# A gated decoder layer on one core: six seven-product places in each half of the down stage with activation sums kept for the second half, and two in each half of the output stage

## What is computed

```python
x = x + merged @ w_out[i]                      # 2048 x 2048
h2 = rms_norm(x, ln_ffn_w[i])
u = causal_depthwise_conv(h2 @ w_up[i], conv_w[i], conv_b[i])
u_gate, u_val = jnp.split(u, 2, axis=-1)
x = x + (jax.nn.silu(u_gate) * u_val) @ w_down[i]   # 5504 x 2048
h3 = rms_norm(x, ln_ple_w[i])
x = x + jax.nn.sigmoid(h3 @ w_ple_gate[i]) * (p[i] @ w_ple[i])
```

## Time and profile before

| | |
|---|---|
| median of 3 runs | 1422.91 us (1422.76 to 1422.95) |
| profiled execution | 1423.26 us, of it 1421.5 us from the first to the last instruction (its span) |
| TensorE matmuls busy | 1411.3 us, 99% of the span |
| VectorE busy | 1088.8 us, 77% |
| ScalarE busy | 793.7 us, 56% |
| mean granted TensorE clock | 0.999 |

### The profile page before, as it was taken

One profiled execution on the slowest core, in us unless ns is written; L12 is line 12 of the kernel. 1 busy time (PEld: TensorE's weight loads), 2 busy tenths in 40 slices (PEclk: granted clock), 3 DMA queues, 4 the chain that ended last, 5 costly groups with the idle time before them and its releaser, 6 DMA issues.

```text
span 1421.5 us, 19857 instructions
## 1 busy us (share of the span) xinstructions
PE 1411.3 (99%) x7054; PEld 1199.0 (84%) x7054; DVE 1088.8 (77%) x1386; ACT 793.7 (56%) x965; POOL 133.5 (9%) x87
## 2 busy tenths in 40 slices
PE   9999999999999999999999999999999999999997
PEld 7888888888888888888888888888888888888886
DVE  7676767878787888777777777777777888888887
ACT  7565665555455555465555555555555555554654
POOL 0024124100000000001110101101011000000000
PEclk9999999999999999999999999999999999999999
DMA  9655565565665665475656566566665565565663
GB/s 321 204 179 162 162 192 150 162 186 177 201 204 186 219 237 197 157 222 179 194 178 198 185 189 192 177 196 186 192 192 178 199 201 198 173 209 205 215 221 120
DMA packets 190733, 273.48 MB, mean 192 GB/s; under 512 B 11728, under 2 KB 103120, under 8 KB 190544
## 3 DMA queue, kind: packets, MB, share of 16 engines
q1 hardware_dynamic: 190096, 272.04, 59.8%
q10 hardware_dynamic: 576, 0.63, 0.1%
HBM read 270.53 MB, written 2.10 MB: 192 GB/s over the span
## 4 chain that ended last, share of the span: by engine, by line
PE 98%; DVE 1%; DMA 0%; ACT 0%; issue 0%; DVEq 0%; ACTq 0%
PE aux L996 11%; PE main L996 11%; PE main L744 9%; PE main L745 9%; PE main L746 9%; PE aux L1005 6%; PE main L802 6%; PE main L803 6%; PE main L804 6%; PE main L1005 6%; PE aux L802 4%; PE aux L804 4%; PE aux L803 4%; PE aux L745 2%; PE aux L744 2%; PE aux L746 2%
## 5 line engine op out<-in xcount | busy, mean ns | idle before, releaser
L1638 DVE TENSOR_TENSOR w_lo<-raw,w_hi 128x1024 fp32r<-128x1024 f32 (+1 forms) x476 | 581.1, 1235 | 272.4 <-ACT w_hi L1304 271.6
L1304 ACT ACTIVATE w_hi<-raw 128x1024 fp32r<-128x1024 f32 (+1 forms) x476 | 499.4, 1051 | 453.6 <-PE main L746 100.3
L744 PE MATMUL main<-w_hi,xT 128*128 128x512 f32 x446 | 175.8, 394 | 0.3 <-DVE w_lo L2215 0.3
L745 PE MATMUL main<-w_lo,xT 128*128 128x512 f32 x446 | 173.7, 389 | 0.0
L746 PE MATMUL main<-w_hi,xT 128*128 128x512 f32 x446 | 173.6, 389 | 0.0
L996 PE MATMUL aux<-xT,w_hi 128*128 128x512 f32 x704 | 169.7, 391 | 0.0
L996 PE MATMUL main<-xT,w_hi 128*128 128x512 f32 x672 | 162.8, 391 | 0.0
L996 PEld LDWEIGHTS aux<-xT,w_hi 128*128 128x128 f32 x704 | 129.4, 188 | 25.0
L996 PEld LDWEIGHTS main<-xT,w_hi 128*128 128x128 f32 x672 | 123.2, 188 | 23.6
L2340 POOL TENSOR_TENSOR act<-cv 128x512 f32<-128x512 f32 (+1 forms) x22 | 71.8, 3266 | 418.5 <-DVE cv L1880 418.5
L744 PEld LDWEIGHTS main<-w_hi,xT 128*128 128x128 f32 x446 | 83.8, 188 | 17.7 <-DVE xT L1665 1.2
(11 more groups left out here) (381 smaller groups left out, 2250.2 us busy)
## 6 DMA issues: line engine op xcount, KB each, us to landing
raw<-in_w_up SPq DMA_DIRECT2D x336, 256.0 KB
raw<-in_w_in SPq DMA_DIRECT2D x136, 512.0 KB
raw<-in_w_down SPq DMA_DIRECT2D x84, 512.0 KB
raw<-in_w_out SPq DMA_DIRECT2D x32, 512.0 KB
raw<-in_w_ple_gate SPq DMA_DIRECT2D x32, 512.0 KB
raw<-in_w_branch_a SPq DMA_DIRECT2D x16, 512.0 KB
raw<-in_w_branch_b SPq DMA_DIRECT2D x16, 512.0 KB
raw<-in_w_in SPq DMA_DIRECT2D x15, 256.0 KB, 5.8
```

The source lines that it names most:

```text
L744: pe.matmul(acc, th, wh, start=first, stop=False)
L745: pe.matmul(acc, th, wl, start=False, stop=False)
L1304: ac.activation(w_hi[:, u % RING, :, 0:w], raw[:, u % RING, :, 0:w], ACT.Copy).then_inc(hi_full, 1)
L1638: dve.tensor_tensor(w_lo[:, u % RING, :, 0:w], raw[:, u % RING, :, 0:w], w_hi[:, u % RING, :, 0:w].bitcast(F32), ALU.subtract).then_inc(lo ...
```

## The change

- The down stage has places at i = 6, 8, 11, 13, 15, 17 in either half: six where there were five.
- The six activation sums of the first half are kept in buffers of their own (`more_sums_hi`, `more_sums_lo`, 16 KB a partition) and used again in the second half, where none are made.
- The output stage has places at i = 2 and 4 in both halves, with the same two activation sums; before, the second half had i = 3 alone.
- In a VectorE slot the low parts of the weight sums come ahead of `act_sums`.
- In the first unit of an output place the product into `main` comes first, then the wait for the turned block and the product into `aux`. VectorE's low parts of the second turned block ("x1T1") move ahead of the `split_lo` of their slot.
- SBUF: the reserved descriptor scratch goes from its default to 1024 bytes a partition, the filler tile from 312 to 56 floats, to make room.

```diff
-SEVEN_AT = ((5, 8, 11, 14, 17), (5, 8, 11, 14, 17))
+SEVEN_AT = ((6, 8, 11, 13, 15, 17),) * 2
-OUT_AT = ((2, 4), (3,))
+OUT_AT = ((2, 4), (2, 4))
-OUT_FORMS = [2, 4, 3]
+OUT_FORMS = [2, 4]
-        + [DOWN_FORMS + q for q in range(len(SEVENS) - N_GATES - N_OUTS)])
+        + [DOWN_FORMS + SEVEN_AT[p].index(i) for p in range(2) for i in SEVEN_AT[p]]
+        + [DOWN_FORMS + len(SEVEN_AT[0]) + f for f in range(len(LAST_AT))])
-FILL = 312
+FILL = 56
+        more_sums_hi = sb("more_sums_hi", [P, 4, 4, P], F32R, ffn)
+        more_sums_lo = sb("more_sums_lo", [P, 4, 4, P], F32R, ffn)
...
                 if a == 0:
+                    triple(main[:, 0, 0, :], *m_block_t(2 * i + 1, 0), *ring_tile(u, 1), start=False, stop=False)
                     if first:
                         if p:
                             pe.wait_ge(xT_ready, 4 * (NQ + 2))
                         else:
                             pe.wait_ge(gated, 4 * NQ)
-                    triple(gate_product(0), *m_block_t(2 * i, 0), *ring_tile(u, 0), start=first, stop=end)
-                    mm = triple(main[:, 0, 0, :], *m_block_t(2 * i + 1, 0), *ring_tile(u, 1), start=False, stop=False)
+                    mm = triple(gate_product(0), *m_block_t(2 * i, 0), *ring_tile(u, 0), start=first, stop=end)
...
+                if s == out_slot(1) + 1 + X1_LAG[1]:
+                    lo_blocks("x1T1", xT_lo, xT_hi, 4, VCOL["ln_ffn"] + 4, xT_hi_ready, xT_ready, 4 * (NQ + 1))
...
+                for k in range(2):
+                    if s - k in SEVEN:
+                        sums_lo(SEVEN[s - k], k + 1)
                 if s in SUMS_AT:
                     act_sums(SUMS_AT[s])
                 if s + 2 in SEVEN:
                     weight_diffs(s + 2)
                 if s - 1 in SUMS_AT and s - 1 != FIRST_FORM_AT:
                     sums_lo(SUMS_AT[s - 1], 0)
-                for k in range(2):
-                    if s - k in SEVEN:
-                        sums_lo(SEVEN[s - k], k + 1)
...
-    nc = bacc.Bacc("TRN2", target_bir_lowering=False, num_devices=1)
+    nc = bacc.Bacc("TRN2", target_bir_lowering=False, num_devices=1, dynamic_dma_scratch_size=1024)
```

More of the change, by code:

```diff
@@ L158 @@
 SEVEN = {u: q for q, u in enumerate(SEVENS)}
-OUT_FORMS = [2, 4, 3]
+OUT_FORMS = [2, 4]
 DOWN_FORMS = len(GATES_AT) + len(OUT_FORMS)
 FORM = ([f for n in range(1, NQ) for f in range(len(GATES_AT))] + [len(GATES_AT) + OUT_FORMS.index(i) for p in range(2) for i in OUT_AT[p]]
-        + [DOWN_FORMS + q for q in range(len(SEVENS) - N_GATES - N_OUTS)])
+        + [DOWN_FORMS + SEVEN_AT[p].index(i) for p in range(2) for i in SEVEN_AT[p]]
+        + [DOWN_FORMS + len(SEVEN_AT[0]) + f for f in range(len(LAST_AT))])
 N_FORMS = FORM[-1] + 1
 SUMS_AT = {MIX + 2 * UK - 5 + 3 * f: f for f in range(len(GATES_AT))}
-SUMS_AT.update((WOUT + at, len(GATES_AT) + f) for f, at in enumerate([-12, -9, 12]))
-SUMS_AT.update((max(u - 4, DOWN + UK), FORM[q]) for u, q in SEVEN.items() if DOWN <= u < GATE)
+SUMS_AT.update((WOUT + at, len(GATES_AT) + f) for f, at in enumerate([-12, -9]))
+SUMS_AT.update((max(u - 4, DOWN + UK), FORM[q]) for u, q in SEVEN.items() if DOWN <= u < DOWN + 2 * UD)
 SUMS_AT.update((GATE + at, N_FORMS - len(LAST_AT) + f) for f, at in enumerate([6, 10]))
@@ L480, in form_place @@
         def form_place(f):
+            if DOWN_FORMS + 2 <= f < N_FORMS - len(LAST_AT):
+                return f - DOWN_FORMS + 1
             return 2 if f == 2 else f % 2
@@ L487, in form_parts @@
                 return [t[:, KD - 4:KD - 2, :].rearrange("p k (h t) -> p (k h) t", t=P) for t in (mT_hi, mT_lo)]
-            return a_sums_hi[:, f % 2], a_sums_lo[:, f % 2]
+            if form_place(f) > 2:
+                return more_sums_hi[:, form_place(f) - 3], more_sums_lo[:, form_place(f) - 3]
+            return a_sums_hi[:, form_place(f)], a_sums_lo[:, form_place(f)]
         def form_before(f):
-            return max(e for e in range(f) if form_place(e) == form_place(f))
+            return max((e for e in range(f) if form_place(e) == form_place(f)), default=None)
         def down_acc(n, tb):
@@ L1460, in sums_hi @@
                     ac.wait_ge(a_summed, q + 1)
-                    if q >= len(GATES_AT):
+                    if form_before(q) is not None:
                         ac.wait_ge(w_sums_done, 2 * max(r + 1 for r in range(len(SEVENS)) if FORM[r] == form_before(q)))
@@ L1919, in join_parts @@
                 else:
-                    u = SEVENS[FORM.index(f)]
-                    k, hi, lo = u - DOWN - 2 * UD * (u >= DOWN + 2 * UD), aT_hi, aT_lo
+                    k, hi, lo = 2 * SEVEN_AT[0][f - DOWN_FORMS], aT_hi, aT_lo
                 if f == DOWN_FORMS:
@@ L2179, in slot @@
                                 inverse_rms(norm)
-                        if s == at + 1 + (2, X1_LAG[n])[norm == 1]:
+                        if s == at + 1 + (2, X1_LAG[n])[norm == 1] and name != "x1T1":
                             lo_blocks(name, xT_lo, xT_hi, 4 * n, VCOL[vec] + 4 * n, xT_hi_ready, xT_ready, 4 * (NQ * norm + n))
```

## The result

The changed kernel takes 1426.08 us (median of 11 runs, 1425.58 to 1426.60), the kernel before, in runs taken beside it, 1422.93 (1422.76 to 1423.40). The ratio is 1.0022, with a 95% interval from 1.0014 to 1.0030: slower, by 3.15 us in the medians. The profiled execution took 1426.32 us, with a span of 1424.5; that of before had 1423.26 and 1421.5.

The account below looks back on a forecast made before the run. TensorE was taken to bound the kernel. The terms -2.04 - 0.36 + 4.6 + 0.9 gave +3.1 us on the span of 1421.5, thus 1426.4 profiled and a median of 1426.0; range 1422.8 to 1427.8.

Parts of the forecast that it names:

- the down stage +4.6: First down half: holes on TensorE before units 18, 28, 32 and 36 add 4.6 us, bounds 4.0 to 5.2.
- the output stage +0.9: Output stage, second half: holes of 0.5 at the first place and 0.4 before the transposes, bounds 0.3 to 1.4.
- VectorE's 11.39: First down half: VectorE's work in us per four-unit period between places, against TensorE's 10.20.
- the transfer's loop at 11.58: First down half: weight sums to next weight sums through the held transfer takes 11.58 us, if the transfer sets the pace.
- VectorE "without a gap": First down half: sign that VectorE runs gapless over the units with holes, a period's steps taking 11.4 us.
- E + 11.68: E is when TensorE ends unit 11; weight sums of the place at 16 end 11.68 us later, releasing unit 20's transfer.
- The sign on the transfer: Down stage: the forecast is wrong if a transfer lands later than 4.3 us after the sums.
- The second half: Second down half: no holes, bounds 0 to 0.8; transfer loop 2.3 us too long against 2.5 us of work gone.
- VectorE keeps up (1): Rival: VectorE's period is 10.20 or less, no new hole in the down stage, 1420.5 to 1420.9 us; chance 0.06.
- the lead absorbs half (2): Rival: VectorE reaches the place at 22 a unit (2.72 us) ahead of the count, giving 1423.0 us; chance 0.14.
- The second half falls behind (4): Rival: the second down half's 2.3 us come out in full, 1428.3 us; chance 0.07.
- The clock (3): Rival: holes of about 1.2 us each 10 us cost TensorE's higher clock, near 1436 us; chance 0.03.

Follow-up runs that it names:

- experiment 4: Changed kernel, but the second down half makes its own activation sums, four units ahead of each place: 1430.71 us, ratio 1.0054 to the kernel before.
- Experiment 7: Changed kernel with all six places per down half four units apart (pairs 7, 9, 11, 13, 15, 17) and activation sums in other slots: 1427.20 us.
- experiment 6: Kernel before with only the small DMA scratch and the filler of 56 columns: 1423.06 us against 1423.02.
- experiments 2: Changed kernel, same places, with the first down half's activation sums made in earlier slots: 1425.81 us, ratio 1.0021 to the kernel before.
- experiments 5 to 8: Against the changed kernel, 5 moves two output-stage steps: 1425.06 us; 8 adds spread places and other sum slots: 1420.21 us. 6 and 7 have their own lines.

## Why the prediction was right

**The sum.** Forecast 1426.0, measured 1426.08. That it meets to a tenth is in part luck: the changed kernel's own runs scatter over 1.0 us, and the 4.6 for the down stage was taken between 4.4 and 5.0, which the working gave for VectorE alone and for the transfer. The terms are right all the same. Against the trace, with the holes by one distance of starts: matmuls -2.04 (nine, by the page); the old hole -0.36, gone; the down stage +4.6, measured 4.55; the output stage +0.9, measured 0.45 and 0.45 where 0.5 and 0.4 stood. The positions, 18, 28, 32 and 36, are those forecast, and what ends them is `w_lo`.

**The period.** VectorE's 11.39, from distances in the kernel before, came out as 11.54 between weight sums; the 0.15 is a gap ahead of 1161.97 that a transfer ends, through ScalarE. In the profile of experiment 4 the same periods of the first half took 11.42, 11.38 and 11.55. The prediction had counted the transfer's loop at 11.58 and could not tell the two apart. They are as near as it says, and the transfer is a hair's breadth later. Experiment 7 shows the loop on its own.

**VectorE "without a gap".** That sign was put too simply. From 1132.60 to 1134.62 VectorE stands idle, in front of unit 20's tile; the working had this held transfer in it, with the end of sums at E + 11.68 and the next step at E + 17.11. It is the list of signs that forgot it. The sign on the transfer was too sharp in the same way: two of the four transfers above landed 4.32 and 4.38 us after the sums (ends of the sums at 1129.19 and 1144.94), over the 4.3 of the list, while the working had 4.34 up to ScalarE's start.

**Durations and distances.** Between weight sums the trace has 11.54 with the transfer and, less the gap, 11.4 without: the distances of starts were the right measure, since each step of 1.22 is followed 1.14 later. By the Trainium skill, "VectorE: DVE Perf Modes", section "The TRN2 errata", a step of 1024 takes 1.224 us, which the durations of 1.22 again show; summed by it a period would be an estimated 11.96.

**The second half.** No hole, as forecast, but with little to spare. Three of its periods in a row are four units long, and from weight sums to weight sums they took 11.8, 11.0 and 10.8 us against TensorE's 10.20. Behind the last of them `w_lo` of unit 36 ends at 1295.22, and TensorE takes it up at 1295.75; 0.14 of these 0.53 us is what passes in any case:

```profile
1294.00 1.22 DVE L1645 TENSOR_TENSOR w_lo<-raw,w_hi 128x1024 fp32r<-128x1024 f32 x1
...
1295.75 0.39 PE L809 MATMUL aux<-w_hi,aT_hi 128*128 128x512 f32 x1
```

The forecast set what the loop costs against work that no longer stands ahead, and that holds as long as the row of such periods is short; experiment 7 makes it five long and pays 1.5 us. But one sentence there was wrong: that the kept sums gain nothing themselves. With six places per half they are worth 4.6 us (experiment 4). The same working that gave the first half its holes, set on the second half without kept sums, would have said so.

**The rivals.** VectorE keeps up (1), and the lead absorbs half (2): no, the four holes have their full size. The second half falls behind (4): no. The clock (3): the granted clock is 1.00 over all three stages above, that is the higher level of 2.4 GHz, with holes of 1.3 us every 11.5 us, and 1.00 as well over both down halves of experiment 4, which has the longest hole (1.35). The Trainium skill, "TensorE: Matmul & The Clock Gate", section "HAM oscillation", tells of a kernel that loses the level over its waits; in this case none of these holes did that.

**Scratch.** Taken at zero, and zero (experiment 6).

## What to carry to other kernels

Before an edit takes work from the engine that is full, add up what the helping engine does per period of the new pattern and compare it with what the full engine still does; a mean share of 76% did not show what three dense periods in a row cost. Where two loops are near in length (here a helper's work and a transfer that waits for that helper), shortening one gives only the distance to the other, so both have to be measured. And when the work can't be less, place it: the same twelve places and the same steps gave 1424.8 or 1420.2 us, by the slots in which six small sums are made.

## What was not expected of the hardware

One small VectorE step of the activation sums takes 0.29 us everywhere but in two places, and there 1.26: in the kernels of experiments 2 (first) and 7, where it fell beside a product on GpSimd:

```profile
1100.02 0.69 DVE L1935 TENSOR_TENSOR a_sums<-aT_hi,aT_lo 128x512 f32<-128x512 f32 x1
1100.74 1.26 DVE L1944 TENSOR_TENSOR a_sums<-a_sums 128x128 f32<-128x128 f32 x1
...
1099.05 2.81 POOL L2348 TENSOR_TENSOR act<-cv 128x512 f32<-128x512 f32 x1 [20.31 <-DVE cv L1887]
...
1101.34 0.68 DVE L1935 TENSOR_TENSOR a_sums<-aT_hi,aT_lo 128x512 f32<-128x512 f32 x1
1102.06 1.26 DVE L1944 TENSOR_TENSOR a_sums<-a_sums 128x128 f32<-128x128 f32 x1
...
1099.23 3.94 POOL L2348 TENSOR_TENSOR act<-cv 128x512 f32<-128x512 f32 x1 [20.31 <-DVE cv L1887]
```

Both times the step ends 0.14 to 0.15 after the product, and the product ends 1.15 after the VectorE step ahead of it (1100.71 and 1102.02), although one took 2.81 and the other 3.94. In the changed kernel the same product (1097.53, 3.33 long) ends 1.14 after the two `w_lo` that ran beside it, which kept their durations. All three agree with the two engines taking turns: the product waits until VectorE's chain lets go, and the next VectorE step waits for the product. That is read from these rows; no run tests it.

The changed kernel's runs scatter over 1.0 us. The 11 runs of before beside them scatter over 0.6, but the 29 beside experiments 5 to 8 over 1.0 too (1422.70 to 1423.72), so a wider scatter is not shown. A part of it lies ahead of everything that the change touches: the profiles of before and of experiment 6 differ by 0.6 us after the first 80, and by no more than that at the end. The holes' sizes differ between profiles of the same pattern as well (the one at unit 28 was 1.32 in one, 1.25 and 1.02 in others); that a transfer's landing time makes this is only argued.
